# First feed-forward round of a two-block transformer kernel: four up slabs multiplied in quarters of the channels, first norm summed by token

## Chip, cores and metric

The kernel runs as one program on one NeuronCore of a Trainium2 chip. Its metric is the device time of one execution in microseconds (us), taken as the median of several executions. Everything is float32; matrix products run on float32r operands in three passes (see below).

## What is computed

The reference is a transformer block with adaptive modulation, then a second block with attention, retention and a mixture of experts. The change touches only the very first stage: modulation, norm and the first feed-forward layer, for 256 latent tokens `x` and 256 context tokens `ctx` of 1024 channels each.

```python
mx = ada_params(c, w_mod[i], b_mod[i])          # 9 vectors of 1024 for x
x = x + 0.5 * mx[2] * swiglu(modulate(rms_norm(x, norm_g[i, 0]), mx[0], mx[1]),
                             ffn1_w_gu[i], ffn1_w_d[i])
my = ada_params(c_ctx, w_mod[i], b_mod[i])      # the same for ctx
y = y + 0.5 * my[2] * swiglu(modulate(rms_norm(y, norm_g[i, 0]), my[0], my[1]),
                             ffn1_w_gu[i], ffn1_w_d[i])
```

`ada_params` is silu(c) times the 1024 x 9216 matrix `w_mod` plus a bias. Its first third of outputs is needed by the first layer: 1024 shifts (`mx[0]`), 1024 scales (`mx[1]`), 1024 gates (`mx[2]`). `modulate(rms_norm(x, g), shift, scale)` is x * rstd * g * (1 + scale) + shift, with rstd taken over the channels of a token.

## The kernel before

**Layout.** Activations lie with channels on partitions: `xs`, `nhi` and `nlo` hold 8 chunks (k = 0 to 7) of 128 channels by 512 tokens (`BOTH`, context first). A weight matrix comes in slabs of 1024 x 128 (512 KB), four at a time in `raw` (u = 0 to 3). ScalarE rounds a slab to float32r in `hi` (`split_hi`, L1030), VectorE takes the rest in `lo` (`split_lo`, L1553). TensorE multiplies per chunk hi by nhi, hi by nlo and lo by nhi, 24 matmuls of 512 columns for a slab (`slab`, L2491 to L2493; `first_pair`, L2504 to L2506, does two slabs chunk by chunk, waiting for each chunk). A round is four slabs. The feed-forward layer has 11 up rounds in three parts, each followed by two down rounds.

**Modulation.** `w_mod` comes in units of 256 columns (1 MB). Units 0 to 3 are the shifts, 4 to 7 the scales, 8 to 11 the gates of the first layer. For these twelve, TensorE multiplies silu(c) with each unit (`unit_rows`, L2575, 16 matmul records a unit), ScalarE copies four units' rows out of PSUM (`row_copy`, L1085), TensorE turns them to columns (`turn`, L2611), and VectorE adds the bias (`take_mod`, L1813) and forms the gains (`gain_cols`, L1822). A shift and its scale for the same channels are four units apart, so before, all eight units had to be there ahead of the first chunk. The later units are loaded into `modw` during the rounds and summed on VectorE (`mod_job`, L1650 and L1653: 16 instructions for one unit in the first rounds; later jobs partly on ScalarE, L1074).

**The start.** SyncE issues four tiles of `x` and `ctx` (512 KB each, `xraw`), units 0 to 5, slabs 0 and 1, units 6 and 7, slabs 2 and 3, units 8 to 11, then round 1 (L802, L782, L788). TensorE waits for all four tiles and transposes them (L2693), VectorE copies them to `xs` (L1847). ScalarE squares the 8 chunks (L1157), VectorE sums them (L1562, L1565), TensorE sums over the channels with a matrix of ones (L2668, L2671), VectorE takes mean and reciprocal of 128 x 512 (L1766, L1768), ScalarE the root, VectorE multiplies (`x_rstd`, L1855). In between stand the products of the units. Once gains and shifts exist, ScalarE forms `nhi` (`first_hi`, L1209) and VectorE the value and its rest (`first_scale`, L1869; `first_lo`, L1877) chunk by chunk, and TensorE runs slabs 0 and 1 in step with them, then 2 and 3. Products of gate unit 8 stand behind slab 3, of units 9 to 11 behind slabs 0, 2 and 3 of round 1.

**Behind a pair of slabs** ScalarE takes silu of the gate half (L1090), VectorE the product (L1680), both split the hidden chunk (L1094, L1683) and the next round's two slabs, and VectorE does its `mod_job`, in this order. All engines work through their instructions in order; semaphores tie them.

Of the kernel before, what the change touches and what calls it, by code (L numbers as in the profile page):

```python
# [13 lines left out]
P = 128  # L14
# [24 lines left out]
MOD_EARLY = 6  # L39
# [5 lines left out]
BATCH_COPY_AT = {7: 2, 19: 3, 35: 4, 51: 5, 63: 6}  # L45
BATCH_TURN_AT = {10: 2, 22: 3, 38: 4, 54: 5, 66: 6}
BATCH_BANK = (5, 6, 5, 6, 6, 6, 6, 5, 6)
FIRST_QUADS = 3
LATE_ROWS = 7
# [203 lines left out]
def build(nc, t, out):  # L253
# [8 lines left out]
    with ExitStack() as ctx:  # L262
# [26 lines left out]
        macc = sb("macc", 2 * U * MOD_W, at=cst_at + 4 * N_CONST_FIRST)  # L289
# [33 lines left out]
        early_at = [hi_at + MOD_BYTES * m for m in range(4)] + [nhi_at + MOD_BYTES * m for m in range(4)]  # L323
        early_at += [modw_at + MOD_BYTES, modw_at + 3 * MOD_BYTES, region + MOD_BYTES, region + 4 * KD * BOTH + MOD_BYTES]
        mod_early = [sb(f"mod_early{m}", KD * MOD_W, at=early_at[m]) for m in range(MOD_FIRST)]
        vrow = sb("vrow", 3 * P, at=region)
        x_rstd = [sb(f"x_rstd{i}", 4 * BOTH, at=at) for i, at in enumerate((region, modw_at))]
# [125 lines left out]
        in_x = sem("in_x")  # L453
# [9 lines left out]
        x_rows_turned = sem("x_rows_turned")  # L463
        x_turned = sem("x_turned")
# [147 lines left out]
        def row_batch(m):  # L612

            return m // ROW_BATCH if m < MOD_FIRST else LATE_ROWS + (m - MOD_FIRST) // ROW_BATCH

# [4 lines left out]
        def row_unit(m):  # L620

            if m < MOD_FIRST:
                return 0, m, mod_early[m], slot_landed[m], 16
            j = m - MOD_FIRST
            dst = mod_early[4 + j] if j < 4 else modw[:, (j - 4) * KD * MOD_W:(j - 3) * KD * MOD_W]
            return 1, MOD_UNITS - MOD_LATE + j, dst, slot_landed[j], 32
# [152 lines left out]
        def _(sp):  # L779
# [16 lines left out]
            def first_unit(m):  # L796
                mod_unit(0, m, mod_early[m][:, :], slot_landed[m])

            for i, src in enumerate((t["ctx"], t["x"])):

                for h in range(2):
                    sp.dma_start(xraw[:, (2 * i + h) * D:(2 * i + h + 1) * D], src[0, h * P:(h + 1) * P, :]).then_inc(in_x, 16)  # L802
            for m in range(MOD_EARLY):
                first_unit(m)
            for u in range(2):
                first_slab(u)
            for m in range(MOD_EARLY, MOD_NEED):
                first_unit(m)
            for u in range(2, U):
                first_slab(u)  # L810
            for m in range(MOD_NEED, MOD_FIRST):
                if m == MOD_FIRST - 1:
                    sp.wait_ge(x_rows_turned, 8)
                first_unit(m)
# [2536 lines left out]
```

## Time and profile before

| | |
|---|---|
| median of 3 runs | 1891.87 us (1891.34 to 1893.73) |
| the profiled execution | 1891.25 us, of it 1889.5 us span from first to last instruction |
| TensorE busy | 1828.6 us, 97% |
| VectorE busy | 1352.8 us, 72% |
| ScalarE busy | 948.9 us, 50% |
| mean granted TensorE clock | 0.990 |
| read from HBM | 380.45 MB, 202 GB/s over the span |

Matmul records are pipelined: the length of one is longer than its distance to the next, and the distance is what counts in a stream. The granted clock is a share of 2.4 GHz. Chain shares say which engine the end of the run waited for; here 86% of the span is TensorE.

### The profile page before, as it was taken

Reading aid. Unit: us, or ns where it says so; the run is one execution under the profiler, and the core shown is the slowest. Engines: PE = TensorE matmul, PEld = TensorE weight load, DVE = VectorE, ACT = ScalarE, POOL = GpSimd, SP = SyncE. Lnnn points to the kernel's source line nnn. Section 1 sums busy time; section 2 is a strip of 40 time slices with the busy share of each in tenths; the row PEclk is TensorE's granted clock in tenths of the full one; section 3 lists DMA queues with packets and bytes.
Section 4 is the critical chain, followed back from the end, with each engine's and each line's share of the span. In section 5 each row is a group of like instructions: output and inputs, shape, how many; then the busy total and the mean of one; then the engine's idle time right before and its main releaser. Section 6 shows DMA issues by size and latency. Waiting matters only on the chain.

```text
span 1889.5 us, 31556 instructions
## 1 busy us (share of the span) xinstructions
PE 1828.6 (97%) x12123; PEld 1600.3 (85%) x12123; DVE 1352.8 (72%) x1966; ACT 948.9 (50%) x1476; POOL 0.2 (0%) x4
## 2 busy tenths in 40 slices
PE   4999999999999899999999999999999989999997
PEld 3777777776877799999999999999998977777786
DVE  5788999986686766677666666677777763337797
ACT  3325665764345554455445554465555443336675
POOL 0000000000000000000000000000000000000000
PEclk8999999999999999999999999999999989999999
DMA  9857997977411366756665456656655437779894
GB/s 326 238 177 234 286 285 236 296 238 221 118 56 46 91 176 179 200 174 178 182 198 165 135 168 179 199 167 176 170 144 169 146 134 267 269 282 356 297 361 193
DMA packets 516044, 383.21 MB, mean 203 GB/s; under 512 B 13769, under 2 KB 473170, under 8 KB 515794
## 3 DMA queue, kind: packets, MB, share of 16 engines
q1 hardware_dynamic: 515408, 381.25, 65.0%
q8 instruction: 81, 1.33, 0.3%
q14 instruction: 41, 0.34, 0.1%
q10 hardware_dynamic: 514, 0.30, 0.1%
HBM read 380.45 MB, written 1.05 MB: 202 GB/s over the span
## 4 chain that ended last, share of the span: by engine, by line
PE 86%; DVE 5%; DMA 3%; ACT 2%; SPq 2%; issue 1%; DVEq 0%; ACTq 0%
PE ps L2491 18%; PE ps L2493 18%; PE ps L2492 17%; PE ps L3174 3%; PE ps L3176 3%; PE ps L3175 3%; PE ps L2504 2%; PE ps L2505 2%; PE ps L2506 2%; PE ps L3204 2%; PE ps L3202 2%; PE ps L3203 2%; PE ps L3190 1%; DMA modw<-in_w_mod 1%; SPq L782 1%
## 5 line engine op out<-in xcount | busy, mean ns | idle before, releaser
L2491 PE MATMUL ps<-nhi,hi 128*128 128x258 f32 (+2 forms) x1920 | 588.6, 307 | 0.3 <-DVE lo L1553 0.3
L2493 PE MATMUL ps<-nhi,lo 128*128 128x258 f32 (+2 forms) x1920 | 587.3, 306 | 0.0
L2492 PE MATMUL ps<-nlo,hi 128*128 128x258 f32 (+2 forms) x1920 | 585.3, 305 | 0.0
L1553 DVE TENSOR_TENSOR lo<-raw,hi 128x1024 fp32r<-128x1024 f32 (+2 forms) x388 | 460.7, 1189 | 107.5 <-ACT hi L1030 106.7
L1030 ACT ACTIVATE hi<-raw 128x1024 fp32r<-128x1024 f32 (+2 forms) x388 | 395.5, 1024 | 229.6 <-PE ps L2493 174.9
L2491 PEld LDWEIGHTS ps<-nhi,hi 128*128 128x128 f32 x1920 | 363.8, 189 | 26.4 <-issue 7.6
L2493 PEld LDWEIGHTS ps<-nhi,lo 128*128 128x128 f32 x1920 | 363.0, 189 | 16.9
L2492 PEld LDWEIGHTS ps<-nlo,hi 128*128 128x128 f32 x1920 | 362.9, 189 | 16.3
L2491 PE MATMUL ps<-hhi,hi 128*128 128x256 f32 (+1 forms) x576 | 177.3, 308 | 0.0
L2492 PE MATMUL ps<-hlo,hi 128*128 128x256 f32 (+1 forms) x576 | 176.6, 307 | 0.0
L2493 PE MATMUL ps<-hhi,lo 128*128 128x256 f32 (+1 forms) x576 | 176.6, 307 | 0.0
L1110 ACT ACTIVATE sg<-nt,bcol 128x256 f32<-128x256 f32 x66 | 33.6, 509 | 200.5 <-DVE nt L1693 200.4
L1074 ACT ACTIVATE modw<-modw,csil 128x256 f32<-128x256 f32 x264 | 109.9, 497 | 48.3 <-DMA modw<-in_w_mod 48.2
L1670 DVE TENSOR_REDUCE macc<-modw 128x256 f32<-128x1536 f32 x44 | 129.7, 2949 | 1.5
L2491 PEld LDWEIGHTS ps<-hhi,hi 128*128 128x128 f32 x576 | 108.4, 188 | 7.8 <-issue 1.2
L2493 PEld LDWEIGHTS ps<-hhi,lo 128*128 128x128 f32 x576 | 108.4, 188 | 6.1
L2492 PEld LDWEIGHTS ps<-hlo,hi 128*128 128x128 f32 x576 | 108.4, 188 | 5.8
L2350 DVE TENSOR_TENSOR lo<-raw,hi 128x1024 fp32r<-128x1024 f32 x54 | 64.8, 1221 | 47.2 <-ACT hi L1478 46.4
L1757 DVE SCALAR_TENSOR_TENSOR xs<-ps,gcol,xs 128x256 f32<-128x256 f32 x136 | 63.0, 478 | 29.5 <-PE ps L2493 22.4
L3174 PE MATMUL ps<-hi,xghi 128*128 128x512 f32 x176 | 70.8, 402 | 1.2 <-DVE lo L2350 1.2
L3176 PE MATMUL ps<-hi,xglo 128*128 128x512 f32 x176 | 70.5, 401 | 0.0
L3175 PE MATMUL ps<-lo,xghi 128*128 128x512 f32 x176 | 70.2, 399 | 0.0
(423 smaller groups left out, 2942.4 us busy)
## 6 DMA issues: line engine op xcount, KB each, us to landing
raw<-in_ffn_w_gu SPq DMA_DIRECT2D x176, 512.0 KB, 4.7
modw<-in_w_mod SPq DMA_DIRECT2D x56, 1024.0 KB, 7.4
raw<-in_ffn_w_d SPq DMA_DIRECT2D x64, 512.0 KB, 4.3
raw<-in_w_in SPq DMA_DIRECT2D x36, 512.0 KB, 4.6
mod_early<-in_w_mod SPq DMA_DIRECT2D x16, 1024.0 KB, 10.3
raw<-in_w_exp_gate SPq DMA_DIRECT2D x32, 512.0 KB, 6.6
raw_more<-in_w_exp_gate SPq DMA_DIRECT2D x32, 512.0 KB, 7.9
raw<-in_w_exp_up SPq DMA_DIRECT2D x32, 512.0 KB, 7.6
```

The lines of the kernel that those rows point to most:

```text
L1030: nc.scalar.activation(hi[:, u * SLOT:u * SLOT + nk * P], raw[:, u * SLOT:u * SLOT + nk * P], ACT.Copy).then_inc(hi_ready, 1)
L1074: ins = nc.scalar.activation(modw[:, at:at + MOD_W], modw[:, at:at + MOD_W], ACT.Copy, scale=csil[:, k:k + 1])
L1553: v.tensor_tensor(lo[:, s], raw[:, s], hi[:, s].bitcast(F32), ALU.subtract).then_inc(lo_ready, 1)
L1670: v.reduce_sum(acc(u), w[:, rest * MOD_W:].rearrange("p (k n) -> p n k", n=MOD_W), AX_X).then_inc(mod_jobs, 1)
L1757: ins = v.scalar_tensor_tensor(out=x, in0=bank(u, SEQ, at), scalar=col_, in1=x, op0=ALU.mult, op1=ALU.add)
L2350: v.tensor_tensor(ring(False, q), raw_slab(i), ring(True, q).bitcast(F32), ALU.subtract).then_inc(moe_lo, 1)
L2491: pe.matmul(bank(u, T), w_hi(u, k), h_, start=(k == 0), stop=False)
L2492: pe.matmul(bank(u, T), w_hi(u, k), l_, start=False, stop=False)
L2493: ins = pe.matmul(bank(u, T), w_lo(u, k), h_, start=False, stop=(k == nk - 1))
L3174: pe.matmul(o, xh, h_[:, j * 512:(j + 1) * 512], start=(k == 0), stop=False)
L3175: pe.matmul(o, xh, l_[:, j * 512:(j + 1) * 512], start=False, stop=False)
L3176: ins = pe.matmul(o, xl, h_[:, j * 512:(j + 1) * 512], start=False, stop=(k == KD - 1))
```

## The change

- **Order of the loads.** Units come in pairs of shift and scale (0 and 4, 1 and 5, 2 and 6, 3 and 7), with the four slabs between them. The gate units 8 to 11 are loaded among the slabs of round 1 (`gate_units`). The units' places in memory are reassigned.
- **Quarters.** A pair of units gives shift and gain of two chunks (a quarter of the channels). Each quarter has its own row copy, turn, bias, gains (`first_take`) and chunks (`first_chunks`). The batches of rows become 2, 2, 2, 2, 4 units.
- **TensorE's order** is written out: the products of round 0's four slabs go quarter by quarter, in four PSUM banks, with the units' products between them.
- **The first norm** is summed by token: ScalarE squares each raw tile (tokens on partitions) with an accumulated sum, mean, reciprocal and root are of 128 x 4, the root is spread over a diagonal (four 128 x 128 instructions) and sent to all partitions by four matmuls with ones; `x_rstd` reads it from PSUM. Eight squares of 128 x 512, six sums, two norm matmuls and the 128 x 512 reciprocal go. The transposes start tile by tile.
- Semaphore counts are renumbered accordingly.

```diff
-MOD_EARLY = 6
+UNIT_ORDER = (0, 4, 1, 5, 2, 6, 3, 7, 8, 9, 10, 11)
+BATCH_FIRST = (0, 2, 4, 6, 8)
+BATCH_UNITS = (2, 2, 2, 2, 4)
...
@@ SyncE: the loads @@
+            first_unit(0)
+            first_unit(1)
+            first_slab(0)
+            first_unit(2)
+            first_unit(3)
+            first_slab(1)
+            first_slab(2)
+            first_unit(4)
+            first_unit(5)
+            first_slab(3)
+            first_unit(6)
+            first_unit(7)
+
+            def gate_units(idx):
+
+                if idx == U + 1:
+                    first_unit(8)
+                    first_unit(9)
+                if idx == U + 3:
+                    sp.wait_ge(mod_rows, 4)
+                    first_unit(10)
+                    sp.wait_ge(x_products, 8)
+                    sp.wait_ge(x_squared, 4)
+                    first_unit(11)
...
-                            sp.wait_ge(nlo_ready, KD)
+                            sp.wait_ge(mod_rows, 2)
...
@@ ScalarE @@
-            act.wait_ge(x_turned, 8)
-            for k in range(KD):
-                square(0, BOTH, k, 0)
...
+            for i, junk in enumerate((sq, nt, sg, hf)):
+                act.wait_ge(in_x[i], 16)
+                nc.scalar.activation(junk[:, :], xraw[:, i * D:(i + 1) * D], ACT.Square, accum_out=rs[:, i:i + 1]).then_inc(x_squared, 1)
             act.wait_ge(eps_ready, 1)
             nc.scalar.activation(rootc[:, :], epsc[:, :], ACT.Sqrt)
...
+            act.wait_ge(var_ready, 2)
+            nc.scalar.activation(rstd[:, 0:4], rv_[:, 0:4], ACT.Sqrt).then_inc(rstd_ready, 1)
+            act.wait_ge(cols_ready, 1)
+            nc.scalar.activation(csil[:, :], cols[:, 0:16], ACT.Silu)
...
+            row_copy(0)
+            split_hi(0, 0, KD, wait_done=False)
+            for k in (0, 1):
+                first_hi(k)
+            row_copy(1)
+            split_hi(0, 1, KD, wait_done=False)
+            for k in (2, 3):
+                first_hi(k)
+            split_hi(0, 2, KD, wait_done=False)
             split_hi(0, 3, KD, wait_done=False)
+            row_copy(2)
+            for k in (4, 5):
+                first_hi(k)
+            row_copy(3)
+            for k in (6, 7):
+                first_hi(k)
...
@@ VectorE @@
-            for k in range(1, KD - 1):
-                add_square(0, BOTH, k)
-            norm_var(0, BOTH)
+            dve.wait_ge(x_squared, 4)
+            v.tensor_scalar(rs[:, 4:8], rs[:, 0:4], 1.0 / D, EPS, ALU.mult, ALU.add).then_inc(var_ready, 1)
+            dve.wait_ge(var_ready, 1)
+            v.reciprocal(rv_[:, 0:4], rs[:, 4:8]).then_inc(var_ready, 1)
             dve.wait_ge(rstd_ready, 1)
...
+            for i in range(4):
+                v.tensor_scalar(sqsum[:, i * P:(i + 1) * P], const("ident"), rstd[:, i:i + 1], None, ALU.mult).then_inc(x_made, 1)
+            dve.wait_ge(x_products, 9)
...
+            def tokens_root(ks):
+
+                for k in ks:
+                    v.tensor_tensor(x_rstd[k // 4][:, k % 4 * BOTH:(k % 4 + 1) * BOTH], chunk(xs, k), bank(4), ALU.mult)
...
+            tokens_root(range(3))
+            dve.wait_ge(cols_ready, 1)
+            first_take(0)
+            split_lo(0, 0, KD)
+            first_chunks(0)
+            tokens_root(range(3, KD))
+            split_lo(0, 1, KD)
+            first_take(1)
+            first_chunks(1)
+            split_lo(0, 2, KD)
+            split_lo(0, 3, KD)
+            for batch in (2, 3):
+                first_take(batch)
+                first_chunks(batch)
...
@@ TensorE @@
+            unit_rows(0)
+            unit_rows(1)
+            turn(0)
+            ready(0, 0, True)
+            for k in (0, 1):
+                normalised(k)
+                chunks(0, (k,))
+            unit_rows(2)
+            unit_rows(3)
             turn(1)
+            ready(0, 1, True)
+            chunks(1, (0, 1))
+            for k in (2, 3):
+                normalised(k)
+                chunks(0, (k,))
+            chunks(1, (2, 3))
+            ready(0, 2, True)
+            chunks(2, range(4))
+            unit_rows(4)
+            unit_rows(5)
+            ready(0, 3, True)
+            chunks(3, (0, 1))
+            turn(2)
+            chunks(3, (2, 3))
+            for k in (4, 5):
+                normalised(k)
+                chunks(0, (k,))
+            unit_rows(6)
+            unit_rows(7)
+            chunks(1, (4, 5))
+            turn(3)
+            chunks(2, (4, 5))
+            chunks(3, (4, 5))
+            for k in (6, 7):
+                normalised(k)
+                chunks(0, (k,))
+            row_steps(0)
+            for u in range(1, U):
+                chunks(u, (6, 7))
+                row_steps(u)
```

`chunks(u, ks)` is the three matmuls of slab u for each chunk in ks. `first_take(batch)` is two bias additions and two gain instructions for the batch's two chunks; `first_chunks` is `first_scale` and `first_lo` for each of the two.

## Rows read from the trace of the kernel before

**Rows 1.** The page: busy tenths of TensorE, 40 slices of 47.2 us.

```profile
PE   4999999999999899999999999999999989999997
```

**Rows 2.** The windows view: stretch, length, PE, PEld, DVE, ACT, POOL busy, clock, DMA, GB/s.

```profile
20.00:45.00 25.00, 14.90 (x141) 6.92 (x142) 17.07 (x27) 10.90 (x20) 0.00 (x0) 0.72 1.13 332
...
56.00:68.00 12.00, 12.00 (x54) 9.71 (x53) 9.61 (x20) 3.01 (x4) 0.00 (x0) 1.00 1.14 319
200.00:240.00 40.00, 39.73 (x181) 30.80 (x180) 39.76 (x39) 28.15 (x57) 0.00 (x0) 1.00 1.01 299
```

**Rows 3.** The timeline to 31 us: start, length, engine, line, count, [idle before <-releaser].

```profile
9.61 5.67 PE L2693 MATMUL ps<-cst,xraw 128*128 128x128 f32 x32 [9.61 <-DMA xraw<-in_x]
...
13.29 3.19 DVE L1847 COPY xs<-ps 128x512 f32<-128x512 f32 x5 [0.16 <-PE ps L2693]
...
19.15 1.28 ACT L1191 ACT_TABLE_LOAD   x1
...
20.82 3.44 PE L2575 MATMUL ps<-mod_early,csil_rows 128*32 128x256 f32 x32 [5.32 <-ACT csil_rows L1192]
...
26.37 2.80 PE L2575 MATMUL ps<-mod_early,csil_rows 128*32 128x256 f32 x48
```

**Rows 4.** The timeline, 35 to 47.5 us: the last two units and the first product.

```profile
35.21 1.94 PE L2575 MATMUL ps<-mod_early,csil_rows 128*32 128x256 f32 x16 [4.50 <-DMA mod_early<-in_w_mod]
...
38.24 1.94 PE L2575 MATMUL ps<-mod_early,csil_rows 128*32 128x256 f32 x16 [1.10 <-DMA mod_early<-in_w_mod]
...
40.25 0.38 ACT L1085 ACTIVATE mrow<-ps 128x256 f32<-128x256 f32 x1 [7.14 <-PE ps L2575]
...
40.68 1.02 PE L2611 MATMUL ps<-cst,mrow 128*128 128x8 f32 x4 [0.50 <-ACT mrow L1085]
41.74 0.38 DVE L1813 TENSOR_TENSOR modc<-ps,cols 128x16 f32<-128x16 f32 x2 [3.32 <-PE ps L2611]
42.16 0.37 DVE L1822 SCALAR_TENSOR_TENSOR acol<-modc,cols 128x8 f32<-128x8 f32 x2
42.56 5.02 ACT L1209 ACTIVATE nhi<-x_rstd,modc,acol 128x256 fp32r<-128x256 f32 x10 [1.94 <-DVE acol L1822]
...
43.86 0.68 DVE L1877 TENSOR_TENSOR nlo<-nt,nhi 128x512 fp32r<-128x512 f32 x1
44.58 0.74 DVE L1869 TENSOR_SCALAR nt<-x_rstd,acol,modc 128x256 f32<-128x256 f32 x2
...
44.69 0.77 PE L2504 MATMUL ps<-nhi,hi 128*128 128x512 f32 x1 [2.99 <-DVE nlo L1877]
...
47.49 1.04 ACT L1030 ACTIVATE hi<-raw 128x1024 fp32r<-128x1024 f32 x1
```

**Rows 5.** The chain of work that ended last: start, length, what.

```profile
46.31 0.43 PE ps L2504
...
51.22 0.24 PE ps L2504
...
68.60 1.00 PE ps L2575 x16
```

**Rows 6.** The windows view again, in short stretches of the start.

```profile
20.00:22.50 2.50, 1.68 (x16) 0.79 (x20) 1.08 (x2) 2.25 (x6) 0.00 (x0) 0.60 1.10 347
25.00:27.50 2.50, 2.50 (x28) 1.07 (x30) 0.99 (x2) 0.77 (x2) 0.00 (x0) 1.00 1.12 338
32.50:35.00 2.50, 0.00 (x0) 0.00 (x0) 2.50 (x6) 0.61 (x1) 0.00 (x0) 0.83 1.11 349
35.00:37.50 2.50, 1.94 (x16) 0.60 (x16) 2.50 (x4) 0.00 (x0) 0.00 (x0) 0.50 1.13 328
```

**Rows 7.** The timeline of ScalarE and VectorE behind the first slabs.

```profile
57.50 0.60 ACT L1090 ACTIVATE sg<-ps 128x512 f32<-128x512 f32 x1 [3.76 <-PE ps L2506]
...
60.82 1.22 DVE L1553 TENSOR_TENSOR lo<-raw,hi 128x1024 fp32r<-128x1024 f32 x1
...
62.48 5.62 DVE L1653 SCALAR_TENSOR_TENSOR macc<-modw,csil,macc 128x256 f32<-128x256 f32 x14
```

More of the change, by code:

```diff
@@ new lines, in first_take @@
+            def first_take(batch):
+                k0, n = batch_units(batch)
+                dve.wait_ge(mod_first_done, batch + 1)
+                for c in range(2):
+                    ins = v.tensor_tensor(modc[:, 72 * c:72 * c + 2 * KD].rearrange("p (a k) -> p a k", a=2)[:, :, k0:k0 + n],
+                                          modps[:, 2 * k0:2 * k0 + 2 * n, c].rearrange("p (a k) -> p a k", a=2),
+                                          cols[:, B_MOD:B_MOD + 2 * KD].rearrange("p (a k) -> p a k", a=2)[:, :, k0:k0 + n], ALU.add)
+                ins.then_inc(mod_copied, 1)
+                dve.wait_ge(mod_copied, batch + 1)
+                for c in range(2):
+                    ins = v.scalar_tensor_tensor(out=acol[:, 24 * c + k0:24 * c + k0 + n], in0=modc[:, 72 * c + KD + k0:72 * c + KD + k0 + n], scalar=1.0,
+                                                 in1=cols[:, VEC["norm_g"] + k0:VEC["norm_g"] + k0 + n], op0=ALU.add, op1=ALU.mult)
+                ins.then_inc(first_gain, 1)
+                dve.wait_ge(first_gain, batch + 1)
@@ L2632, in up @@
                         for u in range(U):
-                            start = isinstance(i, int) and r0 + i == 0
                             if first and u < 2:
                                 if u == 0:
-                                    first_pair(r0, nk, n_up, nhi, nlo, part_up, late(norm) if T == SEQ else normed(norm), start)
+                                    first_pair(r0, nk, n_up, nhi, nlo, part_up, late(norm))
                             else:
-                                slab(i + r0, u, nk, n_up, nhi, nlo, part_up, start)
+                                slab(i + r0, u, nk, n_up, nhi, nlo, part_up)
                             if mods:
@@ L2641, in ffn @@
                     if mods:
-                        for i in range(rounds):
-                            up(i, th == i == 0)
+                        for i in range(1 if th == 0 else 0, rounds):
+                            up(i)
                     elif th == 0:
@@ L2699, in _, with chunks, normalised @@
             ins.then_inc(vec_turned, 1)
+            for i in range(4):
+                pe.wait_ge(x_made, 8 + i + 1)
+                ins = pe.matmul(bank(4, P, i * P), const("ones"), sqsum[:, i * P:(i + 1) * P], start=True, stop=True)
+            ins.then_inc(x_products, 1)
             pe.wait_ge(csil_ready, 1)
-            for m in range(MOD_NEED):
-                unit_rows(m)
-                if m == 1:
-                    norm_sum(0, BOTH)
-                if m == ROW_BATCH:
-                    turn(0)
-            turn(1)
+            def chunks(u, ks):
+                for k in ks:
+                    h_, l_ = chunk(nhi, k, part=tok(BOTH)), chunk(nlo, k, part=tok(BOTH))
+                    pe.matmul(bank(u), w_hi(u, k), h_, start=(k == 0), stop=False)
+                    pe.matmul(bank(u), w_hi(u, k), l_, start=False, stop=False)
+                    ins = pe.matmul(bank(u), w_lo(u, k), h_, start=False, stop=(k == KD - 1))
+                if k == KD - 1:
+                    ins.then_inc(slab_done, 1)
+            def normalised(k):
+                pe.wait_ge(nlo_ready, k + 1)
+            unit_rows(0)
[7 more added lines that the diff above has]
+            unit_rows(3)
+            turn(1)
+            ready(0, 1, True)
[28 more added lines that the diff above has]
+                row_steps(u)
             ffn("l0f1", BOTH, 0, mods=True)
```

161 lines of the change are left out of this document (71 added, 90 removed).

## The prediction

> **What bounds the kernel now.** I read the page's slices first: TensorE is full nearly everywhere except in the first slice (4 tenths of 47 us) [rows 1]. The windows view then splits the start: from 56 us on TensorE is busy for all of a stretch at clock 1.00, and between 200 and 240 us still 39.73 of 40 us [rows 2]. So what the change can give is the time by which TensorE's run of slabs begins and ends earlier. The timeline to 31 us shows the x tiles landed at 9.61, a table load, and the first unit's product at 20.82, which waited for silu(c) and not for its data [rows 3]. The next timeline shows TensorE waiting for loads: unit 6 landed at 35.21, unit 7 at 38.24; behind the latter stand 1.94 of products, the row copy, the turn, bias and gains, the chunk, and the first slab matmul at 44.69 [rows 4]. The chain puts the end of round 0 at 68.60, where unit 8's product starts (slab 3 is over) [rows 5]. These 68.6 us are what must shrink; everything behind is tied to TensorE's progress, not to absolute times.
>
> **The loads after the change.** From 9.61 to 38.24 nine MB landed (8 units, 2 slabs): 3.2 us a MB, the last unit 3.03 [rows 3, 4]. The new order then lands unit 0 at 12.8, 4 at 16.0, slab 0 at 17.6, units 1 and 5 at 20.7 and 23.9, slabs 1 and 2 at 25.5 and 27.1, units 2 and 6 at 30.3 and 33.5, slab 3 at 35, units 3 and 7 at 38.2 and 41.4. The two slabs more ahead of the last unit cost it 3.2 us, but below nothing waits for it.
>
> **The start.** Only the last tile's two groups of transposes stand behind 9.61 (0.71 each, from 5.67 for eight) and the last copy (0.64, from 3.19 for five): 11.7, and I take 12.3 for the handoffs; before, the copies ran to 16.48 [rows 3]. The accumulating square of a 128 x 1024 tile has no row; the nearest is the 1.04 us copy of that size [rows 4]: four end at about 12.9, a Sqrt table load of 1.28 [rows 3] and two tiny instructions bring the root at 14.6, a Silu table load brings silu(c) at 16.2. When the small vector rows land isn't shown: before, their products stood behind the transposes, which ended at 15.28, without a wait of their own. So silu(c) comes between 16.2 and 18.2. Diagonal (4 x 0.2, from half the 0.37 pitch of a 128 x 256 instruction) and the four broadcast matmuls (0.5 to 1.0 together) lie beside that load. The 3.35 us reciprocal, the squares and sums go, but they lay beside loads: they give only the 4.6 us between 16.2 and 20.82.
>
> **The first quarter.** Two units at the low clock take 3.44 [rows 3]: 19.7. Row copy 0.4, turn 0.9 (1.02 low, 0.35 at the full clock), bias and gains 0.8 [rows 4]: 22.0. VectorE then does slab 0's rest, 1.2 [rows 7], then value 0.72 and rest 0.68 of chunk 0 [rows 4]. **First slab matmul at 24.6 instead of 44.69**, 20 us earlier (26.6 with late vector rows).
>
> **What TensorE has to do from there to the end of slab 3.** Matmuls stand 0.43 apart at the low clock and 0.232 at the full one [rows 5]; 54 in 12 us agree [rows 2]. 96 matmuls: 6 low and 90 full, 23.5. Six units, which before lay in front of 44.69: two at 1.75 and four at 0.95 (2.80 for three [rows 3]), 7.3. Three turns at 0.36, 1.1. Together 31.9, where before 23.9 lay between 44.69 and 68.6.
>
> **What it waits for between.** I walked the three queues in the order of the diff with these durations and 0.05 us a handoff. (a) Row copy of quarter 1: 0.5. (b) ScalarE does row copy 1 and only then rounds slab 1 (1.04), VectorE its rest (1.2): TensorE stands 1.9 at `ready(0, 1)`. (c) Only then come bias, gains and chunks 2 and 3: a step from the end of bias and gains to a chunk is 1.75 (`first_hi` 1.0, then rest 0.7), the next 1.37 later; TensorE waits 1.2 and 0.7. (d) Quarter 2: turn 2 is followed by only six matmuls (1.4), against 0.8 + 1.75: 1.3, and 0.7 for chunk 5. (e) Quarter 3: turn 3 has 12 matmuls (2.8) behind it, 0.5 for chunk 7. Sum 6.8 with the small ones. Units 2 and 6 are wanted at 42.3 and 43.3 and landed at 33.5; 3 and 7 are wanted at 50.7 and 51.6 and landed at 41.4. So the loads no longer set the pace, TensorE's own work and the handoffs do. End of slab 3: 24.6 + 31.9 + 6.8 = 63.3, or 64.5 with late vector rows (part of the delay is absorbed, because more matmuls fall into the full clock). I take the middle, **63.8: 4.8 us before 68.6**.
>
> **What is late next.** Before, the pair 0 and 1 ended 11 us before slab 3 (57.50 against 68.60) [rows 5, 7]; now 2.8 us. The last of slab 1 to the rest of round 1's slab 0 takes 2.9 (silu 0.60, the product of 128 x 512 about 0.7 as a rest of that size, split 1.22, and 0.4 of handoffs) [rows 4, 7]; behind slab 1 stand 2.8 of matmuls and unit 8's 0.95: 0.8 us of cover; gone, each us costs a us. VectorE then does its first `mod_job` (6.2: 5.62 for 14 of its 16 instructions [rows 7]) before the product of slabs 2 and 3, so slab 2 of round 1 is split about 13 us after slab 1's end, and TensorE wants it after 16: 3 us of cover. The gate units, issued behind three to four slabs and the first `modw` unit, land at about 51, 54, 64 and 67; their products stand behind slab 3 (63) and in round 1 (70, 81, 88). SyncE's new waits are for row batches that are done by 31 and 52.6; behind them are only gate units and round 2's slabs, wanted near 89. All edits of counts and banks further on I take at nothing: they rename what is there. From 200 us VectorE is busy 39.76 of 40 [rows 2], but it is fed by TensorE's progress and shifts with it.
>
> **A rule that speaks against it.** TensorE's clock: it was 0.60 on average in 20 to 22.5, where the products started, 1.00 from 25, and after TensorE's stop at 30.7 (4.50 idle before 35.21) it fell, to 0.50 in 35 to 37.5 although 1.94 us of products stood there [rows 3, 4, 6]; the first slab matmuls ran low [rows 5]. I count on the full clock from 29.5, 4.9 us behind the first slab matmul, as it had risen by 25, 4.2 behind 20.82, and on no fall in the walk's gaps, of which none is over 1.9 us. The Trainium skill (TensorE: Matmul & The Clock Gate, "HAM oscillation — how this bites in real kernels") says that bursts of matmuls parted by waits can each run at the lower clock. By that rule the quarters could all run low, which is rival 2.
>
> **Rivals.**
> 1. *A second low stretch.* The pieces between 31 and 37 (gaps of 0.5, 1.9, 1.2 and 0.7 about 5 matmuls' work) let the clock fall until about 41. Price: some 20 matmuls and a unit or two by 0.2 and 0.8, partly in waits: end at 65.0 to 67.0, gain 1.6 to 3.6, time 1888.3 to 1890.3. Speaks for it: the fall after 30.7 and that short products at 35 and 38 did not raise it [rows 6]. Against: that gap was 4.50 us [rows 4].
> 2. *All quarters low* (slower side). 90 matmuls by 0.2, four units by 0.8, turns: 22 us, less absorbed waits 4: end near 81, 12.7 us late, 1904.6. It decides once about 27 more matmuls run low. Against: from 37.5 on the walk has 10 us without a gap.
> 3. *VectorE falls behind.* If the `mod_job` moved in front of slab 2's split came 3 us later than reckoned, each further us costs TensorE one; with 8 us, 1895. Little speaks for it.
> 4. *The gain is given back* before 200 us, where VectorE and the `modw` loads are near full: 1891.9.
>
> **How the numbers follow.** The profiled execution took 1891.25 (span 1889.5), 0.6 below the median of 1891.87; the walk's 4.8 off it gives 1886.5, and off the median 1887.1, which I predict. Forecast (ends 61.1 to 64.7; the low end if the clock is up from 26 on): 1884.4 to 1888.0, chance 0.61. Rival 1: 0.22. Rival 2: 0.06. Rival 3: 0.04. Rival 4: 0.07. The measurement tells 0.2%, 3.8 us, from no change: faster 0.61, same 0.29 (rivals 1 and 4), slower 0.10. The range leaves out rivals 2 and 3 and part of 4: 1884.2 to 1891.2.
>
> **What would show it.** First slab matmul at 24 to 27; clock 1.00 from 30 on; `ready(0, 1)` waiting about 2 us on L1553; no TensorE wait for a unit's load after the first two; unit 8's product at 63 to 65; round 1 without a wait. Wrong if TensorE waits for a load after 30 us, if the clock is 0.50 after 37, or if TensorE's stream shows new gaps between 64 and 90.

## The result, and the profile after

The changed kernel takes **1884.53 us** (median of 6 runs, 1880.04 to 1885.95) against 1892.07 for the kernel before (6 runs, 1889.61 to 1893.73): ratio **0.9957, 95% interval 0.9945 to 0.9968**. By the medians that is 7.5 us faster; 4.8 were forecast. The ratio is estimated from all the executions and isn't the quotient of the two medians, which would be 0.9960. By the ratio, the 1891.87 from which the forecast was made becomes 1883.7 (1881.5 to 1885.8 by its interval): 8.1 us faster, and half a us below the range of 1884.2 to 1891.2. The interval reaches into the range, but not to the 1887.1 that was forecast. The profiled execution took 1884.43 us, of it 1882.7 us span, so its span is 6.8 us shorter than that of before. One execution of `e2_norm_by_channel` below was in a slow state (2704.59 us at a granted clock of 0.618) and is left out of its median.

The slices of the page show the first one at 6 tenths where it was at 4 [rows 1], and the others as before:

```profile
PE   6999999999999899999999999999999989999997
```

The windows view (stretch, length, busy time of PE, PEld, DVE, ACT, POOL, granted clock, DMA share, GB/s), against [rows 2, 6]:

```profile
15.00:20.00 5.00, 3.36 (x44) 2.08 (x42) 2.87 (x9) 2.57 (x6) 0.00 (x0) 1.00 1.13 328
...
22.50:25.00 2.50, 2.17 (x6) 1.26 (x6) 2.40 (x6) 0.00 (x0) 0.00 (x0) 0.64 1.17 300
25.00:27.50 2.50, 2.50 (x30) 1.08 (x32) 1.76 (x3) 0.00 (x0) 0.00 (x0) 0.68 1.16 312
...
30.00:37.50 7.50, 6.88 (x18) 5.36 (x19) 5.55 (x13) 4.09 (x6) 0.00 (x0) 0.54 1.12 334
37.50:62.00 24.50, 22.76 (x146) 15.90 (x144) 8.69 (x23) 7.56 (x14) 0.00 (x0) 1.00 1.12 331
```

Two things are to be seen. In 15 to 20, where the first units' products stand, the clock is 1.00; before, it was 0.60 where they stood [rows 6]. And in 30 to 37.5 it is 0.54, that is near the lower of its two levels, 1.2 GHz, where I had counted on the full one.

TensorE's timeline (start, length, line, count, [idle before <- releaser]) answers to [rows 3, 4]:

```profile
12.85 0.32 PE L2763 MATMUL ps<-cst,vrow 115*128 115x115 f32 x1 [1.84 <-DMA vrow<-in_b_mod]
...
14.66 1.16 PE L2769 MATMUL ps<-sqsum,cst 128*128 128x128 f32 x8 [1.37 <-DVE sqsum L1890]
15.98 1.93 PE L2642 MATMUL ps<-mod_early,csil_rows 128*32 128x256 f32 x32 [0.16 <-ACT csil_rows L1222]
18.41 0.61 PE L2678 MATMUL ps<-cst,mrow 128*128 128x4 f32 x4 [0.50 <-ACT mrow L1112]
22.48 0.47 PE L2777 MATMUL ps<-nhi,hi 128*128 128x512 f32 x1 [3.46 <-DVE nlo L1927]
...
23.83 0.79 PE L2777 MATMUL ps<-nhi,hi 128*128 128x512 f32 x1 [0.33 <-DVE nlo L1927]
...
25.41 2.49 PE L2642 MATMUL ps<-mod_early,csil_rows 128*32 128x256 f32 x32
28.41 0.61 PE L2678 MATMUL ps<-cst,mrow 128*128 128x4 f32 x4 [0.51 <-ACT mrow L1112]
30.62 0.79 PE L2777 MATMUL ps<-nhi,hi 128*128 128x512 f32 x1 [1.60 <-DVE lo L1587]
...
46.90 0.50 PE L2777 MATMUL ps<-nhi,hi 128*128 128x512 f32 x1 [0.95 <-DVE nlo L1927]
...
48.34 0.50 PE L2777 MATMUL ps<-nhi,hi 128*128 128x512 f32 x1 [0.48 <-DVE nlo L1927]
...
56.99 0.50 PE L2777 MATMUL ps<-nhi,hi 128*128 128x512 f32 x1 [0.30 <-DVE nlo L1927]
...
62.04 1.07 PE L2642 MATMUL ps<-mod_early,csil_rows 128*32 128x256 f32 x16
```

The first slab matmul is at 22.48 instead of 44.69, no product waits for a load after 12.85, and unit 8's product, the end of round 0, starts at 62.04 (68.53 in this view before, 68.60 in the chain [rows 5]). The chain, in order of time (start, length, what), walks through the largest wait and shows both distances between matmuls, as [rows 5] did:

```profile
27.98 0.38 ACT mrow L1112
28.36 0.95 ACT hi L1057
29.31 0.02 issue
29.34 1.24 DVE lo L1587
30.57 0.04 issue
30.62 0.79 PE ps L2777
31.41 0.43 PE ps L2778
...
42.53 0.43 PE ps L2777
42.96 0.23 PE ps L2778
```

**Where the gain is.** The end of round 0 moves by 6.5 us. TensorE's matmuls of the second norm's sum are a landmark far behind it: 436.30 before, 430.45 after, 5.9 us. The waits of TensorE from 62 to 430 us (line, releaser, sum, times, longest) explain most of the difference:

```profile
PE ps L2569 <- DVE hlo L1717: 1.3, 1, 1.3
PE ps L2556 <- DVE lo L1587: 0.8, 1, 0.8
```

Before, the same two waits were 1.3 and 0.3. The span falls by 6.8. So the gain is made ahead of 62 us and passed on, with less than 1 us added or lost on the way.

### The profile page after: what moved, and what is told of

Its sections match the earlier page's. It is cut to its first block, busy times and chain, and to the rows that moved or that the text cites. A ratio compares the mean times of both kernels' runs of the same rounds, so it can differ in the third digit from the quotient of the medians.

```text
span 1882.7 us, 31598 instructions
## 1 busy us (share of the span) xinstructions
PE 1830.6 (97%) x12135; PEld 1601.7 (85%) x12135; DVE 1347.2 (72%) x1976; ACT 949.5 (50%) x1477; POOL 0.2 (0%) x4
## 3 DMA queue, kind: packets, MB, share of 16 engines
HBM read 380.45 MB, written 1.05 MB: 203 GB/s over the span
## 4 chain that ended last, share of the span: by engine, by line
PE 87%; DVE 6%; ACT 3%; DMA 2%; issue 2%; ACTq 0%; DVEq 0%; SPq 0%
PE ps L2556 18%; PE ps L2558 17%; PE ps L2557 17%; PE ps L3292 3%; PE ps L3294 3%; PE ps L3293 3%; PE ps L2569 2%; PE ps L2570 2%; PE ps L2571 2%; PE ps L3322 2%; PE ps L3320 2%; PE ps L3321 2%; PE ps L3308 1%; DVE lo L1587 1%; DMA modw<-in_w_mod 1%
## 5 line engine op out<-in xcount | busy, mean ns | idle before, releaser
L2556 PE MATMUL ps<-nhi,hi 128*128 128x258 f32 (+2 forms) x1904 | 581.8, 306 | 0.8 <-DVE lo L1587 0.8
L2558 PE MATMUL ps<-nhi,lo 128*128 128x258 f32 (+2 forms) x1904 | 580.0, 305 | 0.0
L2557 PE MATMUL ps<-nlo,hi 128*128 128x258 f32 (+2 forms) x1904 | 578.3, 304 | 0.0
L1587 DVE TENSOR_TENSOR lo<-raw,hi 128x1024 fp32r<-128x1024 f32 (+2 forms) x388 | 460.7, 1189 | 111.5 <-ACT hi L1057 110.8
L2556 PEld LDWEIGHTS ps<-nhi,hi 128*128 128x128 f32 x1904 | 360.4, 189 | 26.6 <-issue 7.6
L1101 ACT ACTIVATE modw<-modw,csil 128x256 f32<-128x256 f32 x264 | 110.3, 498 | 47.5 <-DMA modw<-in_w_mod 47.3
L1791 DVE SCALAR_TENSOR_TENSOR xs<-ps,gcol,xs 128x256 f32<-128x256 f32 x136 | 63.0, 478 | 29.5 <-PE ps L2558 22.4
L1512 ACT ACTIVATE hi<-raw 128x1024 fp32r<-128x1024 f32 x54 | 56.4, 1060 | 28.0 <-DMA raw<-in_w_exp_up 17.8
```

What stands on the lines that cost most here:

```text
L1101: ins = nc.scalar.activation(modw[:, at:at + MOD_W], modw[:, at:at + MOD_W], ACT.Copy, scale=csil[:, k:k + 1])
L1587: v.tensor_tensor(lo[:, s], raw[:, s], hi[:, s].bitcast(F32), ALU.subtract).then_inc(lo_ready, 1)
L1791: ins = v.scalar_tensor_tensor(out=x, in0=bank(u, SEQ, at), scalar=col_, in1=x, op0=ALU.mult, op1=ALU.add)
L2556: pe.matmul(bank(u, T), w_hi(u, k), h_, start=(k == 0), stop=False)
L2557: pe.matmul(bank(u, T), w_hi(u, k), l_, start=False, stop=False)
L2558: ins = pe.matmul(bank(u, T), w_lo(u, k), h_, start=False, stop=(k == nk - 1))
```

## The experiments

In each table "first" is TensorE's first slab matmul, "end" the start of unit 8's product, both in us, and "stretch" the time between them. The time is a median in us, the ratio that against the kernel before, run beside it on the same chip; "first" and "end" come from one profiled execution each. Before has 44.69, 68.53, 23.8; the changed kernel has 22.48, 62.04, 39.6.

### Each half of the change alone

**Quarters undone** (`e1_all_units_first`): the new loads and the norm by token stay, but all eight units are multiplied first; ScalarE and VectorE follow the same order.

```diff
-            unit_rows(0)
-            unit_rows(1)
-            turn(0)
-            ready(0, 0, True)
-            for k in (0, 1):
-                normalised(k)
-                chunks(0, (k,))
...
+            for b in range(4):
+                unit_rows(2 * b)
+                unit_rows(2 * b + 1)
+                turn(b)
+            for u in range(2):
+                ready(0, u, True)
+            for k in range(KD):
+                normalised(k)
+                for u in range(2):
+                    chunks(u, (k,))
```

> The changed kernel with the quarters undone: new loads and new norm, but TensorE multiplies all eight units before the first slab, then slabs 0 and 1 chunk by chunk, then 2 and 3. Theory A (the gain comes from TensorE multiplying slabs while the units land): the first slab matmul waits for the last unit, which lands near 41.5, and stands near 47; end of round 0 at 71, some 2 to 3 us later than before (two more slabs lie ahead of the last unit), span 1891 to 1893. Theory B (the gain comes from the shorter start, the norm by token, and the quarters only rearrange): end of round 0 at or before 64, span at most 1885.

**Norm by channel again** (`e2_norm_by_channel`): the quarters stay; squares of 128 x 512, their sums, two norm matmuls, the 128 x 512 reciprocal and root come back.

```diff
-                nc.scalar.activation(junk[:, :], xraw[:, i * D:(i + 1) * D], ACT.Square, accum_out=rs[:, i:i + 1]).then_inc(x_squared, 1)
+                nc.scalar.activation(sq[:, (k % 2) * BOTH:(k % 2 + 1) * BOTH], chunk(xs, k), ACT.Square).then_inc(x_squared, 1)
...
-            v.reciprocal(rv_[:, 0:4], rs[:, 4:8]).then_inc(var_ready, 1)
+            v.reciprocal(rv_[:, :], rs[:, :]).then_inc(var_ready, 1)
...
             unit_rows(1)
+            pe.matmul(bank(4), const("ones"), sqsum[:, :], start=True, stop=False)
+            pe.matmul(bank(4), const("ones"), sq[:, BOTH:2 * BOTH], start=False, stop=True).then_inc(x_products, 1)
```

> The changed kernel with the norm undone: eight squares of 128x512, six sums, two norm matmuls, reciprocal and root of 128x512 as before; loads, quarters and orders as changed. Theory A, as I predicted it: the norm by token gives only the 4.6 to 5 us by which silu(c) comes earlier, so the end of round 0 moves from 62.0 to about 68 and the span to 1888 to 1889. Theory C (the reciprocal and root, hidden behind loads before, stand on the path once the first quarter no longer waits for loads): sum at 26.5, reciprocal to 30.5, root, x_rstd, gains, first slab matmul near 36 instead of 22.5, end of round 0 at 72 to 74, span 1892 to 1895, slower than before.

| | first | end | stretch | time | ratio, 95% |
|---|---|---|---|---|---|
| quarters undone | 48.47 | 73.47 | 25.0 | 1895.82 | 1.0018, 1.0009 to 1.0028 |
| norm by channel | 31.89 | 70.40 | 38.5 | 1892.62 | 1.0000, 0.999 to 1.001 |

Neither half gains anything alone; without the quarters the kernel is 3.4 us slower than before. TensorE's timeline then shows the loads in charge, as in [rows 4], and later, since four slabs stand ahead of the last unit instead of two:

```profile
30.77 1.94 PE L2624 MATMUL ps<-mod_early,csil_rows 128*32 128x256 f32 x16 [3.72 <-DMA mod_early<-in_w_mod]
...
48.47 0.77 PE L2759 MATMUL ps<-nhi,hi 128*128 128x512 f32 x1 [3.39 <-DVE nlo L1916]
```

The last unit's product starts at 41.63, as expected, but the first slab matmul is 1.5 us and the end 2.5 us later than expected. No run has the norm by token with the old order of the loads; there TensorE waited until 38.24 for unit 7's load [rows 4], so nothing ahead of that point could have moved the first slab matmul.

Without the norm by token the norm sets the pace. VectorE's timeline and TensorE's:

```profile
22.68 3.35 DVE L1898 RECIPROCAL rv__70<-rs 128x512 f32<-128x512 f32 x1
26.73 1.90 DVE L1904 TENSOR_TENSOR x_rstd<-xs,rstd 128x512 f32<-128x512 f32 x3 [0.70 <-ACT rstd L1239]
...
31.89 0.76 PE L2781 MATMUL ps<-nhi,hi 128*128 128x512 f32 x1 [9.63 <-DVE nlo L1935]
```

The units' products start at 16.30 there too, so it isn't silu(c) that is late: the sums, the reciprocal and the root are, and they put the first slab matmul 9.4 us and the end 8.4 us behind the changed kernel's, or 8.4 and 6.6 us behind those of its second profiled execution below (23.54 and 63.76). The ratios (1.0000 against 0.9957 and 0.9963) say 8.1 and 7.0 us. So of the theories the one with the norm on the path holds, at a smaller size than its first slab matmul near 36 and its end at 72 to 74: by token, the norm is worth 6.6 to 8.4 us inside the quarters, not the 4.6 that the prediction gave it.

### Does a later start cost its whole length?

`e5_silu_late` puts five copies of a 128 x 1024 tile in front of silu(c) on ScalarE. The load of unit 11, far behind, waits for silu(c) instead of the squares.

```diff
-                    sp.wait_ge(x_squared, 4)
+                    sp.wait_ge(csil_ready, 1)
...
+            for _ in range(5):
+                link(nc.scalar.activation(hf[:, :], xraw[:, 3 * D:4 * D], ACT.Copy))
             nc.scalar.activation(csil[:, :], cols[:, 0:16], ACT.Silu)
```

> The changed kernel with five linked copies of 128x1024 on ScalarE in front of silu(c): its units start near 21 instead of 15.98, as late as before the change, and TensorE idles as long. Theory A: every us passes on to the end, and the two units run at the low clock (3.44 instead of 1.93), the turn too: first slab matmul at 29 to 30, end of round 0 at 68 to 69.5, span 1888.5 to 1890. Theory D (the waits between the quarters absorb a late start): end of round 0 at 64 to 65, span 1885.

Measured: first 30.29, end 69.82, stretch 39.5, time 1890.89, ratio 0.9990 (0.998 to 0.9999). TensorE's timeline:

```profile
21.66 3.64 PE L2644 MATMUL ps<-mod_early,csil_rows 128*32 128x256 f32 x32 [5.46 <-ACT csil_rows L1224]
...
30.29 0.76 PE L2779 MATMUL ps<-nhi,hi 128*128 128x512 f32 x1 [3.46 <-DVE nlo L1929]
```

The units started 5.7 us later (21.66), took 3.64 at the low clock instead of 1.93, and the turn 1.02 instead of 0.61: that is the 7.8 us by which the first slab matmul came later, and the end came 7.8 later. Nothing of a later start was absorbed.

### Does the clock hold the stretch back?

`e4_hold_clock` puts matmuls on constants, whose result nothing reads, into two gaps.

```diff
+            def hold(n):
+                for _ in range(n):
+                    pe.matmul(bank(3, 128), const("ones"), cst[:, 0:128], start=True, stop=True)
...
             turn(0)
+            hold(11)
...
             turn(1)
+            hold(5)
```

> The changed kernel with extra matmuls that nothing reads (ones by constants, 128 columns, into bank 3) after turn 0 (11) and turn 1 (5), so that TensorE has no stop there. Theory A (the stretch at the low clock from 23.8 to 36.7 comes from the stops at 19 to 22.5 and 29 to 30.6): the clock stays at 1.00 from 16 us on, 18 matmuls get 0.2 us shorter each, units 2 and 3 0.55 together, less what becomes waiting for VectorE: end of round 0 at 59 to 60.5, span 1879.5 to 1881.5. Theory E (the clock falls whatever stands there): no change, end at 62, span 1882.7.

Measured: first 24.80, end 61.86, stretch 37.06, time 1881.86, ratio 0.9938 (0.9921 to 0.9955). The windows view has the clock at full speed where the changed kernel had 0.54:

```profile
30.00:37.50 7.50, 6.04 (x29) 4.41 (x30) 6.37 (x13) 4.47 (x7) 0.00 (x0) 1.00 1.12 334
```

The low clock behind the first slab matmul thus cost the changed kernel 2.5 us of its stretch. This execution's first slab matmul came 2.3 us later than the changed kernel's, on units of 3.64 us, and it still ended 0.2 earlier. The expectation had reckoned with a clock of 1.00 from 16 us on; it was 0.50 from 15 to 20, and so the end at 59 to 60.5 was missed.

### The same kernel again

`e0_changed_again` is the changed kernel, unedited. Its first slab matmul had stood at 22.48, that of `e4_hold_clock`, with the same instructions up to turn 0, at 24.80, and nothing in the edit explained it.

> The changed kernel itself, word for word, once more. Theory F (the clock at 15 to 20 us differs between executions: 1.00 in the changed kernel's trace, 0.50 in that of the kernel with extra matmuls, though both run the same instructions until then): in an execution with the low clock there the first slab matmul stands at 24.6 to 24.9 instead of 22.48 and round 0 ends at 63.5 to 65 instead of 62.04; in one with the full clock both repeat. Theory G (the clock there follows from the code alone): 22.5 and 62.0 again. Time in either case 1883 to 1886.

Measured: first 23.54, end 63.76, stretch 40.2, time 1885.30, ratio 0.9963 (0.995 to 0.9975). The time repeats; the start doesn't. Timeline and windows:

```profile
14.54 2.07 PE L2769 MATMUL ps<-sqsum,cst 128*128 128x128 f32 x8 [1.63 <-DVE sqsum L1890]
16.55 2.40 PE L2642 MATMUL ps<-mod_early,csil_rows 128*32 128x256 f32 x32
...
27.50:30.00 2.50, 2.50 (x28) 0.81 (x20) 0.32 (x1) 0.00 (x0) 0.00 (x0) 0.50 1.09 350
```

The broadcast matmuls took 2.07 (1.16 in the other execution) and the units 2.40 (1.93): the same instructions behind nearly the same wait (1.63 and 1.37), at another clock. This execution was the slowest of its five (1886.92, median 1885.30). Its end lies in the 63.5 to 65 expected for the low clock, its first slab matmul between the two cases: the clock of one program differs between executions, and its start moves with it.

### The waits in the stretch

`e3_slab1_split_early` rounds slab 1 ahead of the row copy:

```diff
-            row_copy(1)
             split_hi(0, 1, KD, wait_done=False)
+            row_copy(1)
```

> The changed kernel, but ScalarE rounds slab 1 before row copy 1 instead of behind it. Theory A (TensorE stood 1.60 us at slab 1's rest because ScalarE did the row copy first): from the first slab matmul to the end of round 0 38.0 to 38.6 us instead of 39.56, the wait on the rest of slab 1 gone or under 0.3; span 1 to 1.5 less than a changed kernel with the same clock at the start. Rival (slab 1 lands only near 28, so the row copy behind it comes late): no change.

`e6_units_earlier` puts more matmuls between a turn and the chunks that need it:

```diff
             chunks(1, (2, 3))
+            unit_rows(4)
+            unit_rows(5)
             ready(0, 2, True)
             chunks(2, range(4))
-            unit_rows(4)
-            unit_rows(5)
+            turn(2)
             ready(0, 3, True)
-            chunks(3, (0, 1))
-            turn(2)
-            chunks(3, (2, 3))
-            for k in (4, 5):
-                normalised(k)
-                chunks(0, (k,))
+            chunks(3, range(4))
+            normalised(4)
+            chunks(0, (4,))
             unit_rows(6)
+            normalised(5)
+            chunks(0, (5,))
             unit_rows(7)
...
-            for k in (6, 7):
-                normalised(k)
-                chunks(0, (k,))
+            normalised(6)
+            chunks(0, (6,))
+            chunks(1, (6,))
+            normalised(7)
+            chunks(0, (7,))
```

> The changed kernel, but TensorE multiplies units 2 and 6 ahead of slab 2, turns them behind it, and puts units 3 and 7 and a chunk of slab 1 where it waited for chunks 4, 5 and 7 (0.95, 0.48 and 0.30 us). Theory A (TensorE's order sets the pace from 37 us on and no load does): these waits go, first slab matmul to end of round 0 37.7 to 38.2 us instead of 39.56. Rival (the loads set it): units 2, 6 land after 34 and 3, 7 after 41, a wait for mod_early appears instead, 39 to 40 us.

`e7_three_together` is these two and the matmuls of `e4_hold_clock`.

> Extra matmuls behind turns 0 and 1 (they took 2.5 us off the stretch from first slab matmul to end of round 0: 37.06 instead of 39.56), slab 1 rounded early, and units multiplied earlier, together. If the three savings add up: 34.3 to 35.5 us for the stretch, end of round 0 at 57 to 60 by the clock at the start, median 1878 to 1881, ratio 0.9915 to 0.9935. Rival (the extra matmuls behind turn 1 now stand in the way, as slab 1 is ready): 36 us, median as with the extra matmuls alone, 1881.9.

| | first | end | stretch | time | ratio, 95% |
|---|---|---|---|---|---|
| slab 1 rounded early | 23.98 | 61.45 | 37.5 | 1886.18 | 0.9963, 0.995 to 0.9975 |
| units earlier | 23.73 | 60.01 | 36.3 | 1881.21 | 0.9951, 0.9936 to 0.9967 |
| all three | 23.85 | 57.37 | 33.5 | 1878.34 | 0.9929, 0.9916 to 0.9942 |

Each shortens the stretch, by 2.1, 3.3 and, together, 6.0 us, each time a little more than expected. The clock has a part in it, since from 22.5 to 62 it was 0.91 and 0.89 where the changed kernel had 0.87, and 1.00 with all three. The savings add up only in part: 2.5, 2.1 and 3.3 would be 7.9. With slab 1 early the 1.60 at L2777 is gone, but waits of 0.95 and 0.49 for chunks 2 and 3 take part of its place. With the units earlier the waits of 0.95, 0.48 and 0.30 are gone. All three together beat both kernels, the changed one by 7.0 us (1885.30 for `e0_changed_again`, run beside them). The time with the units earlier is less sure: four of its six executions took 1878.3 to 1881.9, two 1886.7 and 1887.6. Slab 1's early rounding doesn't show in the time at all. Its profiled execution, the slowest of its five, loses the gain again far behind round 0; its windows view:

```profile
620.00:640.00 20.00, 17.51 (x72) 13.47 (x72) 7.33 (x14) 2.08 (x5) 0.00 (x0) 0.58 0.09 28
```

The changed kernel has 0.90 there:

```profile
620.00:640.00 20.00, 16.00 (x93) 12.57 (x93) 9.42 (x18) 4.21 (x11) 0.00 (x0) 0.90 0.17 51
```

From end to the last instruction are 1824.3 us there against 1820.7 in the changed kernel and 1818.4 in `e7_three_together`. The 3.6 us are lost between 620 and 660 us: ScalarE's root of the norm there (L1188) stands 602.2 us behind the end (663.64), in the changed kernel 598.7 (660.75), while TensorE's first matmul of L3008 still stood 1.0 us nearer (558.4 against 559.5). That the other four executions of this kernel lost time in the same way isn't shown.

### The clock of the start, in both kernels

`b1_before_again` is the kernel before, unedited. `b2_before_clock_held` puts matmuls on constants into its three gaps.

```diff
             for m in range(MOD_NEED):
                 unit_rows(m)
...
+                if m == 5:
+                    hold(17)
+                if m == 6:
+                    hold(8)
             turn(1)
+            hold(11)
```

> The kernel before, word for word, once more. It shows how much its own start differs between executions. If only the changed kernel's start depends on the clock of the execution: first slab matmul at 44.5 to 44.9 and round 0's end at 68.4 to 68.8 again, span 1889 to 1891. If before's does too: an end that differs by 1 us or more from 68.60.

> The kernel before with extra matmuls that nothing reads wherever TensorE waited for units 6 and 7 and for the first chunk. Theory A (part of before's late end is the low clock of 35 to 48 us): unit 7's products 0.93 instead of 1.94, the turn 0.35 to 0.6 instead of 1.02, first slab matmul at 43.0 to 43.4 instead of 44.69, its first seven matmuls 0.2 us shorter each, end of round 0 at 65.3 to 66.3 instead of 68.60, ratio 0.998 to 0.999. Rival (the extra matmuls only heat the gaps, the chain is VectorE's): end at 68.

`e9_clock_held_11_to_16` does it to the changed kernel between the transposes and the broadcast; `e8_clock_held_from_11` is this with `e7_three_together`.

```diff
+            def warm(n):
+                for _ in range(n):
+                    pe.matmul(bank(5, 128), const("ones"), cst[:, 0:128], start=True, stop=True)
+            warm(6)
             pe.wait_ge(in_vec, 16 * N_VEC_DMAS)
...
+            warm(4)
             for i in range(4):
                 pe.wait_ge(x_made, 8 + i + 1)
```

> The changed kernel with extra matmuls only between its transposes and the sum over the tokens (11 to 14.6 us). If what I mis-sized is the clock of the first two units (3.44 us in my sum, 1.93 and 2.40 in the two traces of the changed kernel): units in 1.93 to 2.0, first slab matmul at 22.3 to 22.8 in this execution too, end of round 0 at 61.5 to 62.5, median 1883.5 to 1885. Rival (the clock at 16 us is set by something else): units at 3.4 or between, first slab matmul over 23.5.

> All together: the clock held from 11 us on, extra matmuls behind turns 0 and 1, slab 1 rounded early, units multiplied earlier. The stretch from first slab matmul to end of round 0 as in the kernel with three together (33.5 us), but the first slab matmul at 22.4 to 22.8 instead of 23.85: end at 55.9 to 56.5, median 1876.5 to 1878, ratio 0.991 to 0.993.

| | first | end | stretch | time | ratio, 95% |
|---|---|---|---|---|---|
| before again | 44.39 | 69.01 | 24.6 | 1892.46 | 1.0009, 1.0000 to 1.0018 |
| before, clock held | 43.03 | 65.46 | 22.4 | 1888.28 | 0.9987, 0.9978 to 0.9996 |
| changed, held 11 to 16 | 22.45 | 60.41 | 38.0 | 1882.18 | 0.9956, 0.9942 to 0.9970 |
| held, with all three | 22.53 | 56.26 | 33.7 | 1880.24 | 0.9940, 0.9927 to 0.9954 |

Before repeats in its time; its end is 0.5 us later, less than the 1 us that was to tell a dependence on the execution. Its ratio also shows what two samples of one and the same kernel can differ by: 0.0009. Holding the clock of before moves its end by 3.1 us (65.46 from 68.53), as units 6 and 7 take 1.07 instead of 1.94 [rows 4]:

```profile
34.81 1.07 PE L2575 MATMUL ps<-mod_early,csil_rows 128*32 128x256 f32 x16
...
37.86 1.07 PE L2575 MATMUL ps<-mod_early,csil_rows 128*32 128x256 f32 x16
```

Some 3 us of the start of the kernel before were therefore clock, against the 6.5 of the change. The change isn't that in another form: with matmuls on constants in both kernels the end still moves by 5.1 us, from 65.46 to 60.41. In both kernels with matmuls from 11 us on, the first two units take 1.93; TensorE's timeline of `e9_clock_held_11_to_16`:

```profile
14.62 1.16 PE L2776 MATMUL ps<-sqsum,cst 128*128 128x128 f32 x8 [0.56 <-DVE sqsum L1890]
15.94 1.93 PE L2642 MATMUL ps<-mod_early,csil_rows 128*32 128x256 f32 x32 [0.16 <-ACT csil_rows L1222]
```

The changed kernel with its first units held ended at 60.41, earlier than the 61.5 to 62.5 expected, since more of the stretch ran at the full clock as well (0.96 from 22.5 to 62, for 0.87). Its ratio isn't told apart from the unedited kernel's 0.9957 and 0.9963. The last kernel has the earliest end of all, 56.26, 1.1 before `e7_three_together`, but its span of 1878.6 is 2.8 longer: 1822.3 us follow the end. Its median misses the 1876.5 to 1878 expected and isn't told apart from `e7_three_together`'s, as the intervals overlap. Of the 3.9 us more behind the end, 1.9 are two waits of TensorE, for the rests of L1587 (1.4 for 0.5) and for `hf` (L2460, 1.7 for 0.7); the clock from 1480 to 1580 was 0.93 for 0.95. Why these waits grew, and where the rest lies, stays open.

## Why the prediction was right in kind and short in size

**What held.** *The place of the gain*: all in the first 62 us. *The loads*: nothing waits for them after the start. *silu(c)*: reckoned between 16.2 and 18.2, the products started at 15.98, because the vector rows had landed by 12.85. *The norm's root*: Sqrt table, root, Silu table follow each other as walked. *What is late next*: nothing; round 1 starts right behind unit 8 at 63.04, and its first `mod_job` (5.63) lies beside products. Rival 3 is out. So is rival 4: span minus end is 1821.0 before and 1820.7 after. Rival 2 is out: 37.5 to 62 at clock 1.00. The Trainium skill's rule of bursts that each run at the lower clock (TensorE: Matmul & The Clock Gate, "HAM oscillation — how this bites in real kernels") was borne out only in part: the clock was low for the matmuls from 23.83, behind idle times of 3.46 and 0.33, and from 30.62, behind 1.60; the later ones, behind 0.95, 0.48 and 0.30, ran at full clock. Of the signs that were to show the forecast, three failed: the first slab matmul stood ahead of its 24 to 27, the clock wasn't 1.00 from 30 on, and unit 8's product stood ahead of 63.

**The step that failed: the first quarter.** "Two units at the low clock take 3.44" was taken from [rows 3], where ScalarE had held TensorE for 5.32 us. After the change TensorE has the small products and the broadcast in front, with idle times of 1.84, 1.37 and 0.16, and in the profiled execution the units took 1.93. The term is 1.5 us too large; the turn, 0.9 in the sum, took 0.61, and bias and gains took 0.5 for 0.8, silu(c) was 0.2 early, and the steps from the gains to the first slab matmul took 2.85 for 2.6. Together 2.1, and 24.6 becomes 22.5. The idle times alone don't explain the clock, as six other executions with the same instructions up to there had 2.40 to 3.64. So 3.44 lay among the values that the units can take; the step went wrong in taking one of them as fixed. I had moreover set the end half a us later for late vector rows, which weren't late; and `e5_silu_late` shows that such a delay isn't absorbed in part, as I had it (24.6 to 26.6 giving 63.3 to 64.5), but passed on whole.

That this term is the cause for the profiled execution is measured, but it isn't a constant of the kernel, and of the six timed executions only this one shows its units. `e0_changed_again` ended at 63.76, my own 63.8, with the units at 2.40 and more low clock behind them. That the ends agree is luck: its first slab matmul stood at 23.54 and its stretch was 40.2, not 24.6 and 38.7. The ratio of its five runs was still 0.9963. Part of the difference lies on the side of before: its profiled execution, 1891.25, from which the forecast's distance to the median was taken, lies 0.2 to 1.2 under the five medians of that kernel (1892.07, 1892.38, 1891.98, 1891.49, and 1892.46 in `b1_before_again`), while the 1884.43 of after lies 0.1 under its own. Of the 7.5 us, 6.5 are the end of round 0 and 0.3 what follows up to the last instruction; the other 0.7 is the distance of the profiled execution of before to the median of its six runs, less the 0.1 of after. The ratio adds 0.6. So of the 3.3 us between 4.8 and 8.1, 1.7 come from the end of round 0. That end, 62.04, lies within the 61.1 to 64.7 of the forecast; what carried the time out of the range is the rest, the spread between executions above all, for which no step of the walk had a term.

**The stretch: 38.7 forecast, 39.6 measured, by errors that cancelled.** From 24.6 to 63.3 stood 31.9 of work and 6.8 of waits.
- *Waits*: 4.2 (0.33 for chunk 1, 0.51 row copy, 1.60, 0.95, 0.48, 0.30). Row copy (a) and slab 1's rest (b) came as walked, 0.5 and 1.6 for 0.5 and 1.9; the waits for chunks 2 and 3 (c) did not show, since the matmuls ahead ran slowly; at full clock, in `e9_clock_held_11_to_16`, they were 0.61 and 0.48 for 1.2 and 0.7. Chunks 4 and 5 (d) were 1.43 for 2.0, chunk 7 (e) 0.30 for 0.5.
- *Low clock*: about 17 of the 96 matmuls stood 0.43 apart, 6 had been reckoned: 11 x 0.2 = 2.2 more. This is rival 1, at about its place (30.6 to 36.8) and its price, and it came beside an early start, which hid it. `e4_hold_clock` measures its removal at 2.5.
- *Units*: six took 6.2 (2.48, 1.86, 1.86 in the chain) for 7.3; two turns of 0.35 and one of 0.61 took 0.2 more than the 1.1.
- *Restarts*, which the sum left out: the first matmul behind a wait or behind another tile shape counts 0.43 to 0.79 in the chain where 0.23 or 0.43 is the distance in the stream. Over the nine of the stretch that is some 2.1 us; only the sum of all terms shows it, no run changed it alone.
- 31.9 + 2.2 - 1.1 + 0.2 + 2.1 = 35.3, and with 4.2 of waits 39.5.

**The norm.** "They give only the 4.6 us between 16.2 and 20.82" was wrong as a price, though it entered the sum nowhere else. It was read from a kernel in which the norm lay beside loads. In the order of the change nothing is left beside which it could lie: `e2_norm_by_channel` measures 6.6 to 8.4.

**The range** had its lower end at 1884.2. For it I had let the clock be up from 26 on, but not at the first units; with their 1.5 and the 0.3 of the turn it would have held the time.

## What to carry to other kernels

Of a step that "lies beside the loads", ask what it lies beside in the new order; here two halves that each gained nothing alone (1.0018 and 1.0000) gave 0.9957 together. Price a short product after a gap at both clocks and carry both ends into the range, since one program can show either at the same instruction; where gaps remain on the path, a few matmuls on constants are a cheap trial (here 2.5 us of the stretch, and 3.1 in the kernel before). In a stretch that is cut into pieces, count the restarts too.

## What the runs showed that I had not expected

- The granted clock at one instruction differs between executions of the same program: the broadcast took 1.16 and 2.07, the two units behind it 1.93 and 2.40, the next two 2.49 and 3.64 in two executions of the changed kernel. In kernels that are the same up to this point the two units took 1.93, 2.40, 2.45, 3.36, 3.39, 3.47 and 3.64. The Trainium skill (TensorE: Matmul & The Clock Gate, "What's actually happening") says that the number of slow matmuls at a kernel's start varies from run to run; the executions agree (2.49 and 3.64), and not for the start alone. What decides it, the runs don't show; with extra matmuls from 11 us on it was 1.93 in both kernels tried, in one profiled execution each.
- Every trace has stretches of low clock far behind the start. From 620 to 640 us it was 0.58 to 0.93, but for `e1_all_units_first`, where it came only behind 640 (0.91 to 660). What follows round 0 varies between 1818 and 1824 us, nearly as much as this change gains. The clock there accounts for that in `e3_slab1_split_early` alone: traces with 0.83 in that window have 1818.1, 1818.4, 1821.0 and 1822.3 us behind the end.
- The square with an accumulated sum costs ScalarE 1.04 us for 128 x 1024, as a plain copy of that size does [rows 4]; the reading of the accumulator (0.19 in the records) overlaps it, so that four follow each other 1.05 apart.
